# Block one's output projection: divided beside the attention stream, or whole behind it

## The chip, the cores and the metric

One NeuronCore of one Trainium2 chip runs the whole program. The metric is the device time of one execution in microseconds (us), the median of the runs shown. TensorE (PE in the profile) multiplies, VectorE (DVE), ScalarE (ACT) and GpSimd (POOL) do the rest, SyncE (SP) issues the weight loads.

## The reference

Two transformer blocks of two layers each run on 512 tokens of width 1024, in float32. The change lies in block one, whose layer is

```
h    = rmsnorm(x, norm_attn)
proj = h @ w_in
o    = concat(stick_breaking(4 heads), moba(4), nsa(4), diff(4))   # 512 x 1024
x    = x + o @ w_out
x    = x + square(relu(rmsnorm(x, norm_mlp) @ w_up)) @ w_down
```

Block two (SwiGLU, a mixer with pooling, convolution and neighbourhood attention, SwiGLU, each with a layer norm) is the same before and after.

## The kernel before

**Layout.** The activations are held transposed: `xT[:, k, :]` is chunk k of 128 channels by 512 tokens. Each product is done in three matmuls on rounded parts, weight high x input high, weight high x input low, weight low x input high (`three`, L628), so each weight piece (128 x 1024, 8 blocks of 128 x 128) is split: ScalarE copies the high part (`high_for`, L1139), VectorE subtracts for the low part (`split_for`, L1605). Pieces go through four slots in one fixed order; SP loads a piece into its slot when VectorE has split the one before it (L471). `high_for(n)` and `split_for(n)` prepare the piece that follows piece n in its slot. `wait_ge` and `then_inc` on semaphores order the engines; inside an engine all goes in program order.

**The attention stream.** 48 units (head pair and query tile; the width is one to four key tiles of 128) are worked off in 51 steps, an order written out by hand for each engine. At step i TensorE does `scores(i)` (L772), `values(i - 3)` (L811) and `turn(i - 2)`, the transposes (L784). VectorE adds the bias and takes the maximum (`add_bias(i)`, L1760) and scales the exponentials (`weigh(i - 1)`, L1801); ScalarE takes the exponentials (`exponential(i)`, L1253) and copies the transposed probabilities out of PSUM (`turned_out(i - 2)`, L1070). So a unit goes through all three engines and back in three steps. When all units of a stage (a head pair) are done, VectorE copies its output to a chunk of `mixT` (L1805). ScalarE and VectorE then make the chunk's high part (`mix_high`, L1281, at the steps of `HIGH_STEP`) and low part (`mix_low`, L1833, at those of `LOW_STEP`), which the projection reads. The sub-norm of the differential heads' chunks 6 and 7 is the product at L1872.

**The fill.** Between the small matmuls of a step TensorE does large ones. First the last ten pieces of the input projection (`STREAM`), in thirds of 9, 9 and 6 matmuls at the steps of `THIRD_STEP` (L171): the last third, of k5, is at step 37. Then the first part of the output projection at the steps of `HALF_STEP` (L179): for each of eight output chunks d, five of its eight input chunks (`OUT_A`), 15 matmuls in halves of 9 and 6, at steps 40 to 51; the last two halves (step 51) follow the stream. VectorE adds each group to `xT` (`add_group`, L1836), which frees the PSUM bank; two banks, `acc[0]` and `acc[1]`, serve in turn.

**Behind the stream** come eight groups of the other three input chunks (`OUT_B`), 9 matmuls each, each again with an addition. Behind the addition ScalarE and VectorE make the scaled high and low parts (L1325, L1848) that the MLP's first group (`group`, L537, L532 to L534) reads, ScalarE squares the chunk (L1330) and POOL adds the squares (L2202). The weights of the projection are packed on the host in the order of their use (L2326).

Of the kernel before, what the change touches and what calls it, by code (L numbers as in the profile page):

```python
# [25 lines left out]
P = 128  # L26
# [67 lines left out]
GP_MLP = 12 + NC  # L94
# [76 lines left out]
THIRD_STEP = [2 * x for x in range(8)] + [16 + x * 8 // 11 for x in range(11)] + [24 + x * 15 // 11 for x in range(11)]  # L171
# [5 lines left out]
OUT_A, OUT_B = 5, 3  # L177
assert OUT_A + OUT_B == NC
HALF_STEP = [40 + y * 11 // 14 for y in range(2 * NC)]  # L179


def half_from(y):
    return y // 2 * OUT_A + (3 if y % 2 else 0)


def closes_piece(y):
    return half_from(y + 1) // NC > half_from(y) // NC


HIGH_STEP = [37, 37, 38, 38, 39, 47, 47]  # L190
LOW_STEP = [38, 38, 39, 39, 39, 47, 48]
# [20 lines left out]
def emit(nc, x_in, weights, const_in, bucket_in, par1_in, par2_in, table_in, rpb_in, out):  # L212
    with ExitStack() as ctx:
# [3 lines left out]
        def sem(name):  # L217
            return ctx.enter_context(nc.semaphore(name))
# [181 lines left out]
        scaled_hi, scaled_lo, out_done = sem("scaled_hi"), sem("scaled_lo"), sem("out_done")  # L400
# [123 lines left out]
        def _(pe):  # L524
# [109 lines left out]
            def attention(layer):  # L634
# [182 lines left out]
                def out_group(d, order, first_block, first_piece, m):  # L817

                    pe.wait_ge(evacuated[m % 2], gp + m // 2)
                    for n, k in enumerate(order):  # L820
                        block = first_block + n
                        index = R_ATT * SLOTS + first_piece + block // NC
                        if block % NC == 0 or n == 0:
                            pe.wait_ge(split_done, done + (index + 1))
                        if d == 0:
                            pe.wait_ge(mix_lo, layer * NC + (MIX_ORDER.index(k) + 1))
                        w = slice(block % NC * P, (block % NC + 1) * P)
                        mm = three(acc[m % 2][:, :], index % SLOTS, w, k, n == 0, n == len(order) - 1)
                        if block % NC == NC - 1:
                            mm.then_inc(pieces_done, 1)  # L830
                        if n in (2, len(order) - 1):
                            yield
                    if d < NC - 1:
                        mm.then_inc(out_done, 1)

                def first_outs():
                    for d in range(NC):
                        yield from out_group(d, MIX_ORDER[0:OUT_A], d * OUT_A, 0, 24 + d)

                fill, outs = pieces(STREAM), first_outs()  # L840
                for i in range(N_STEPS):
                    if i < N_UNITS:
                        scores(i)
                    thirds, halves = THIRD_STEP.count(i), HALF_STEP.count(i)
                    if thirds > 0:
                        next(fill)
                    elif halves > 0:
                        next(outs)
                    if i >= 3:
                        values(i - 3)  # L850
                    for _ in range(thirds - 1):
                        next(fill)
# [215 lines left out]
        def _(act):  # L1068
# [66 lines left out]
            def attention(layer):  # L1135
# [147 lines left out]
                for i in range(N_STEPS):  # L1283
# [30 lines left out]
                    for y, step in enumerate(HALF_STEP):  # L1314
                        if i == step + 1 and closes_piece(y):
                            high_for(R_ATT * SLOTS + half_from(y) // NC)
                mix_high(NC - 1)
                for y, step in enumerate(HALF_STEP):
                    if step + 1 >= N_STEPS and closes_piece(y):
                        high_for(R_ATT * SLOTS + half_from(y) // NC)  # L1320
                gps = layer * GPS1 + (GP_SETUP + 12 + NC // 2)
                for k in range(NC):
# [9 lines left out]
                    if (k + 1) * OUT_B // NC > k * OUT_B // NC:  # L1332
                        high_for(R_ATT * SLOTS + OUT_A + k * OUT_B // NC)
# [165 lines left out]
        def _(dve):  # L1499
# [101 lines left out]
            def attention(layer):  # L1601
# [234 lines left out]
                def add_group(group):  # L1836
                    m, d = 24 + group, group % NC
                    if d < NC - 1:
                        dve.wait_ge(out_done, layer * (2 * NC - 2) + (group // NC * (NC - 1) + d + 1))
                    else:  # L1840

                        dve.wait_ge(pieces_done, layer * (ROUNDS1 * SLOTS) + R_ATT * SLOTS + (NC if group >= NC else OUT_A))
                    dve.tensor_tensor(xT[:, d, :], acc[m % 2][:, :], xT[:, d, :], ALU.add).then_inc(evacuated[m % 2], 1)  # L1843
# [8 lines left out]
                for i in range(N_STEPS):  # L1852
# [24 lines left out]
                    for y, step in enumerate(HALF_STEP):  # L1877
                        if i == step + 1 and y % 2:
                            add_group(y // 2)
                        if i == step + 2 and closes_piece(y):  # L1880
                            split_for(R_ATT * SLOTS + half_from(y) // NC)
                for y, step in enumerate(HALF_STEP):
                    if y == 2 * NC - 1:
                        mix_low(NC - 1)
                    if step + 1 >= N_STEPS and y % 2:
                        add_group(y // 2)
                    if step + 2 >= N_STEPS and closes_piece(y):
                        split_for(R_ATT * SLOTS + half_from(y) // NC)
# [399 lines left out]
def _pieces(inputs):  # L2288
# [10 lines left out]
    for l in range(DEPTH):  # L2299
# [26 lines left out]
        for order in (MIX_ORDER[0:OUT_A], MIX_ORDER[OUT_A:]):  # L2326
            tiles = [w_out[k * P:(k + 1) * P, d * P:(d + 1) * P] for d in range(NC) for k in order]
            for n in range(0, len(tiles), NC):
                out.append(np.stack(tiles[n:n + NC], 1).reshape(-1))
# [97 lines left out]
```

## Time and profile before

| what | us |
|---|---|
| median of 3 runs (3367.01 to 3369.91) | 3369.19 |
| the profiled execution's own time | 3365.77 |
| its span from first to last instruction | 3363.8 |
| PE busy, of the span | 3278.3 |
| DVE busy | 2049.4 |
| ACT busy | 715.2 |
| POOL busy | 288.7 |
| mean granted TensorE clock | 0.993 |

The profile is of one execution, with times from the first instruction. A row of the timeline gives start and length; neighbouring instructions of one kind are merged (x8), and TensorE's matmuls overlap, so their pace is the distance of their starts, not their length. A number in brackets is the idle time before, with what ended it. Clock 1.00 is 2.4 GHz, 0.50 is 1.2 GHz. The scores of block one (L772) run from 132.6 to 327.4 us in layer one and from 829.0 to 1020.6 in layer two.

### The profile page before, as it was taken

The numbers are of one execution on the slowest core, as the hardware profiler recorded it, in microseconds if no ns is written. First come the engines' busy times: TensorE is split into PE (matmuls) and PEld (weight loads), VectorE is DVE, ScalarE is ACT, GpSimd is POOL, SyncE is SP. The second block draws the span as 40 slices with busy tenths as digits, with TensorE's granted clock in tenths as the row PEclk, the third lists the DMA queues.
The fourth block names the chain that finished last, engine by engine and source line by source line (L and its number), as shares of the span: only waits on it lengthen the run. The fifth ranks groups of instructions, "written<-read, shape, count | busy, mean of one in ns | idle before, by whom it ended". The sixth has DMA issues, their size and how long they took to land.

```text
span 3363.8 us, 44654 instructions
## 1 busy us (share of the span) xinstructions
PE 3278.3 (97%) x15358; PEld 2585.0 (77%) x15358; DVE 2049.4 (61%) x3166; ACT 715.2 (21%) x1419; POOL 288.7 (9%) x224
## 2 busy tenths in 40 slices
PE   8999999999999999999999999999999999999998
PEld 6766788878657888788886778888788867778886
DVE  5676655555776555654457776455745476774547
ACT  3465200014653000100003321000200023320001
POOL 0110100030101000200002410000100014200001
PEclk9999999999999999999999999999999999999999
DMA  5211223224112222232322213222222222222222
GB/s 215 94 45 51 91 94 100 94 76 150 39 57 72 97 97 95 87 99 96 100 81 94 70 63 100 100 95 86 95 94 94 95 79 90 65 86 98 96 95 68
DMA packets 86777, 302.20 MB, mean 90 GB/s; under 512 B 9267, under 2 KB 10035, under 8 KB 86368
## 3 DMA queue, kind: packets, MB, share of 16 engines
q1 hardware_dynamic: 81180, 287.67, 25.5%
q10 hardware_dynamic: 5444, 12.52, 1.1%
q8 instruction: 91, 1.49, 0.2%
q14 instruction: 62, 0.51, 0.0%
HBM read 298.03 MB, written 6.06 MB: 90 GB/s over the span
## 4 chain that ended last, share of the span: by engine, by line
PE 88%; DVE 5%; DVEq 3%; issue 2%; ACT 1%; DMA 1%; POOL 1%; POOLq 0%; ACTq 0%; SPq 0%
PE acc L532 19%; PE acc L534 19%; PE acc L533 19%; PE acc L630 3%; PE acc L631 2%; PE acc L632 2%; PE acc L879 2%; PE acc L881 2%; PE acc L880 2%; PE score L772 2%; PE outp L811 1%; PE trans L784 1%; DVE wL L1509 1%; PE acc L562 1%; PE acc L563 1%
## 5 line engine op out<-in xcount | busy, mean ns | idle before, releaser
L1509 DVE TENSOR_TENSOR wL<-wraw,wH 128x1024 fp32r<-128x1024 f32 x459 | 605.1, 1318 | 34.3
L533 PE MATMUL acc<-opL,wH 128*128 128x512 f32 x1280 | 498.2, 389 | 0.0
L532 PE MATMUL acc<-opH,wH 128*128 128x512 f32 x1280 | 498.2, 389 | 0.0
L534 PE MATMUL acc<-opH,wL 128*128 128x512 f32 x1280 | 498.2, 389 | 0.0
L532 PE MATMUL acc<-hidH,wH 128*128 128x512 f32 x1072 | 417.2, 389 | 0.0
L534 PE MATMUL acc<-hidH,wL 128*128 128x512 f32 x1072 | 417.2, 389 | 0.0
L533 PE MATMUL acc<-hidL,wH 128*128 128x512 f32 x1072 | 417.2, 389 | 0.0
L1507 DVE CAST wH<-wraw 128x1024 fp32r<-128x1024 f32 x459 | 324.8, 708 | 135.4 <-PE acc L534 121.4
L1405 ACT ACTIVATE big<-acc 128x512 f32<-128x512 f32 x84 | 50.5, 601 | 1173.1 <-PE acc L534 1170.2
L534 PEld LDWEIGHTS acc<-opH,wL 128*128 128x128 f32 x1280 | 240.4, 188 | 50.0
L532 PEld LDWEIGHTS acc<-opH,wH 128*128 128x128 f32 x1280 | 240.4, 188 | 49.8
L533 PEld LDWEIGHTS acc<-opL,wH 128*128 128x128 f32 x1280 | 240.4, 188 | 49.5
L1990 DVE TENSOR_TENSOR xT<-acc,xT 128x512 f32 (+1 forms) x128 | 88.3, 690 | 266.2 <-PE acc L534 253.9
L534 PEld LDWEIGHTS acc<-hidH,wL 128*128 128x128 f32 x1072 | 201.3, 188 | 42.0
L533 PEld LDWEIGHTS acc<-hidL,wH 128*128 128x128 f32 x1072 | 201.3, 188 | 41.6
L532 PEld LDWEIGHTS acc<-hidH,wH 128*128 128x128 f32 x1072 | 201.3, 188 | 41.5
L2017 DVE SCALAR_TENSOR_TENSOR big<-acc,big 128x512 f32<-128x512 f32 x84 | 58.0, 691 | 276.1 <-PE acc L534 275.7
L532 PE MATMUL acc<-scaledH,wH 128*128 128x512 f32 x512 | 201.5, 394 | 3.9 <-DVE xT L1843 3.9
L630 PE MATMUL acc<-opH,wH 128*128 128x512 f32 x448 | 189.9, 424 | 11.1 <-DVE xT L1843 5.4
L534 PE MATMUL acc<-scaledH,wL 128*128 128x512 f32 x512 | 200.6, 392 | 0.0
L533 PE MATMUL acc<-scaledL,wH 128*128 128x512 f32 x512 | 200.6, 392 | 0.0
L632 PE MATMUL acc<-opH,wL 128*128 128x512 f32 x448 | 178.3, 398 | 0.0
(310 smaller groups left out, 4955.2 us busy)
## 6 DMA issues: line engine op xcount, KB each, us to landing
wraw<-in_weights SPq DMA_DIRECT2D x507, 512.0 KB, 3.3
wraw<-in_weights SPq DMA_DIRECT2D x32, 384.0 KB, 3.0
big<-bias_scratch ACTq DMA_DIRECT2D x10, 512.0 KB, 3.6
bias_scratch<-bias_rows SPq DMA_DIRECT2D x3, 1280.0 KB
big<-in_par ACTq DMA_DIRECT2D x2, 1536.0 KB, 8.0
big<-in_x SPq DMA_DIRECT2D x4, 512.0 KB, 8.9
mixT<-bias_scratch ACTq DMA_DIRECT2D x2, 1024.0 KB, 7.7
out_x<-big SPq DMA_DIRECT2D x8, 256.0 KB, 2.3
```

Source lines behind the costliest of these rows:

```text
L532: pe.matmul(accum[:, :], wH[:, slot, w], hi[:, k, :], start=k == 0, stop=False)
L533: pe.matmul(accum[:, :], wH[:, slot, w], lo[:, k, :], start=False, stop=False)
L534: mm = pe.matmul(accum[:, :], wL[:, slot, w], hi[:, k, :], start=False, stop=k == n - 1)
L630: pe.matmul(accum, wH[:, slot, w], hi[:, k, :], start=first, stop=False)
L631: pe.matmul(accum, wH[:, slot, w], lo[:, k, :], start=False, stop=False)
L632: return pe.matmul(accum, wL[:, slot, w], hi[:, k, :], start=False, stop=last)
L772: pe.matmul(scp[b][:, 0:width], q[rows_of, x.t * P:(x.t + 1) * P], k[rows_of, 0:width], start=True, stop=True).then_inc(scores_ready, 1)
L879: pe.matmul(accum, wH[:, slot, w], opH[:, k, :], start=k == 0, stop=False)
L880: pe.matmul(accum, wH[:, slot, w], opL[:, k, :], start=False, stop=False)
L1507: dve.tensor_copy(wH[:, slot, :], wraw[:, slot, :])
L1509: dve.tensor_tensor(wL[:, slot, :], wraw[:, slot, :], wH[:, slot, :].bitcast(F32), ALU.subtract).then_inc(split_done, 1)
L1990: ins = dve.tensor_tensor(x, acc[j % 2][:, :], x, ALU.add)
```

## The change

The output projection is no longer divided. Steps 42 to 50 of the stream have no fill. Behind the stream come eight groups of 24 matmuls, one for each output chunk and weight piece, in the order `MIX_ORDER` of the input chunks, with one addition each: eight additions per layer where there were sixteen. The thirds of the last pieces of the input projection are set from `24 + x * 15 // 11` to `24 + x * 17 // 10`, so v5 ends at step 30 (29 before), q5 at 35 (33), k5 at 41 (37). The high and low parts of `mixT` move from steps 37 to 39 to steps 42 to 45, the last ones stay about where they were. The weight pieces of the projection are packed whole, one for each output chunk; their number and size are the same. The semaphore `out_done` goes; the additions wait for `pieces_done`.

```diff
-GP_MLP = 12 + NC
+GP_MLP = 12 + NC // 2
...
-THIRD_STEP = [2 * x for x in range(8)] + [16 + x * 8 // 11 for x in range(11)] + [24 + x * 15 // 11 for x in range(11)]
+THIRD_STEP = [2 * x for x in range(8)] + [16 + x * 8 // 11 for x in range(11)] + [24 + x * 17 // 10 for x in range(11)]
...
-OUT_A, OUT_B = 5, 3
-assert OUT_A + OUT_B == NC
-HALF_STEP = [40 + y * 11 // 14 for y in range(2 * NC)]
...
-HIGH_STEP = [37, 37, 38, 38, 39, 47, 47]
-LOW_STEP = [38, 38, 39, 39, 39, 47, 48]
+HIGH_STEP = [42, 42, 43, 43, 44, 47, 47]
+LOW_STEP = [43, 43, 44, 44, 45, 48, 48]
...
+                def out_group(d):
+
+                    index, m = R_ATT * SLOTS + d, 24 + d
                     pe.wait_ge(evacuated[m % 2], gp + m // 2)
+                    pe.wait_ge(split_done, done + (index + 1))
+                    for n, k in enumerate(MIX_ORDER):
                         if d == 0:
+                            pe.wait_ge(mix_lo, layer * NC + (n + 1))
+                        mm = three(acc[m % 2][:, :], index % SLOTS, slice(n * P, (n + 1) * P), k, n == 0, n == NC - 1)
+                    mm.then_inc(pieces_done, 1)
...
-                    thirds, halves = THIRD_STEP.count(i), HALF_STEP.count(i)
+                    thirds = THIRD_STEP.count(i)
                     if thirds > 0:
                         next(fill)
-                    elif halves > 0:
-                        next(outs)
...
-                    for _ in range(halves if thirds else halves - 1):
-                        next(outs)
...
                 rest_of(fill)
-                rest_of(outs)
                 for d in range(NC):
-                    rest_of(out_group(d, MIX_ORDER[OUT_A:], d * OUT_B, OUT_A, 24 + NC + d))
+                    out_group(d)
...
-                    if (k + 1) * OUT_B // NC > k * OUT_B // NC:
-                        high_for(R_ATT * SLOTS + OUT_A + k * OUT_B // NC)
+                    high_for(R_ATT * SLOTS + k)
...
+                def add_group(d):
+                    m = 24 + d
+                    dve.wait_ge(pieces_done, layer * (ROUNDS1 * SLOTS) + (R_ATT * SLOTS + d + 1))
                     dve.tensor_tensor(xT[:, d, :], acc[m % 2][:, :], xT[:, d, :], ALU.add).then_inc(evacuated[m % 2], 1)
...
+                mix_low(NC - 1)
                 for d in range(NC):
-                    add_group(NC + d)
+                    add_group(d)
                     if d > 0:
                         scaled_low(d - 1)
-                    last = (d + 1) * OUT_B // NC > d * OUT_B // NC
-                    if last and d < NC - 1:
-                        split_for(R_ATT * SLOTS + OUT_A + d * OUT_B // NC)
+                    if d < NC - 1:
+                        split_for(R_ATT * SLOTS + d)
                 scaled_low(NC - 1)
...
+        for d in range(NC):
+            tiles = [w_out[k * P:(k + 1) * P, d * P:(d + 1) * P] for k in MIX_ORDER]
+            out.append(np.stack(tiles, 1).reshape(-1))
```

## Rows read from the trace of the kernel before

**Rows 1.** The page: shares of the chain that ended last, by engine.
```profile
PE 88%; DVE 5%; DVEq 3%; issue 2%; ACT 1%; DMA 1%; POOL 1%; POOLq 0%; ACTq 0%; SPq 0%
```

**Rows 2.** Windows: length, busy (count) of PE, PEld, DVE, ACT, POOL; clock, DMA share, GB/s.
```profile
985.05:1036.64 51.59, 49.84 (x284) 33.63 (x285) 31.65 (x94) 26.09 (x67) 0.00 (x0) 0.97 0.17 52
1036.64:1060.12 23.48, 20.32 (x89) 16.21 (x88) 17.58 (x21) 11.32 (x17) 7.11 (x5) 1.00 0.20 68
1060.12:1067.29 7.17, 7.17 (x25) 5.72 (x26) 5.23 (x5) 3.18 (x5) 3.05 (x2) 0.76 0.30 87
291.70:343.40 51.70, 49.63 (x284) 33.56 (x284) 31.65 (x94) 26.10 (x67) 0.00 (x0) 0.97 0.16 52
366.88:374.03 7.15, 7.15 (x25) 5.72 (x25) 5.32 (x5) 3.27 (x5) 3.06 (x2) 0.76 0.25 83
```

**Rows 3.** Timeline, PE, steps 46 and 47: start, length, engine, line, what [idle before <- releaser].
```profile
1014.47 1.09 PE L784 MATMUL trans<-const,big 128*128 128x128 f32 x8
1015.49 0.92 PE L772 MATMUL score<-big 64*128 64x384 f32 x4
1016.34 0.50 PE L630 MATMUL acc<-opH,wH 128*128 128x512 f32 x1
...
1018.62 1.09 PE L811 MATMUL outp<-big 128*64 128x128 f32 x16
1019.65 0.44 PE L784 MATMUL trans<-const,big 128*128 128x128 f32 x2
1020.01 1.13 PE L772 MATMUL score<-big 64*128 64x512 f32 x4
```

**Rows 4.** Timeline, PE, the divided projection's waits and the first MLP group.
```profile
1030.12 0.50 PE L630 MATMUL acc<-opH,wH 128*128 128x512 f32 x1 [1.52 <-DVE xT L1843]
...
1049.92 0.39 PE L631 MATMUL acc<-opL,wH 128*128 128x512 f32 x1
1050.15 0.39 PE L632 MATMUL acc<-opH,wL 128*128 128x512 f32 x1
1051.70 0.50 PE L630 MATMUL acc<-opH,wH 128*128 128x512 f32 x1 [1.16 <-DVE xT L1843]
...
1060.12 0.47 PE L532 MATMUL acc<-scaledH,wH 128*128 128x512 f32 x1 [2.00 <-DVE xT L1843]
```

**Rows 5.** Timeline, PE, steps 39 and 40.
```profile
983.49 0.40 PE L811 MATMUL outp<-big 128*64 128x128 f32 x2 [1.34 <-ACT big L1070]
...
985.05 1.13 PE L772 MATMUL score<-big 64*128 64x128 f32 x4 [0.78 <-DVE small L1760]
```

**Rows 6.** Windows, steps 38 to 40, columns as in rows 2.
```profile
978.89:982.10 3.21, 3.21 (x18) 1.59 (x17) 1.87 (x9) 2.96 (x6) 0.00 (x0) 1.00 0.01 3
982.10:985.98 3.88, 1.63 (x10) 0.99 (x8) 3.75 (x10) 3.88 (x10) 0.00 (x0) 1.00 0.01 2
986.00:989.30 3.30, 3.20 (x9) 1.98 (x7) 3.15 (x6) 2.01 (x6) 0.00 (x0) 0.50 0.02 5
```

**Rows 7.** Timeline, ACT: projection copy, weight copy, exponential of four tiles, two high parts.
```profile
983.25 0.58 ACT L1070 ACTIVATE big<-acc 128x512 f32<-128x512 f32 x1
983.73 1.05 ACT L1070 ACTIVATE wH<-wraw 128x1024 fp32r<-128x1024 f32 x1
...
1002.75 0.72 ACT L1253 ACTIVATE big<-big,small 128x512 f32<-128x512 f32 x1 [0.55 <-DVE small L1760]
...
1026.23 1.15 ACT L1070 ACTIVATE opH<-mixT 128x512 fp32r<-128x512 f32 x2
```

**Rows 8.** Timeline, DVE: stage copy, sub-norm product, addition, bias of four tiles.
```profile
1019.79 0.69 DVE L1805 TENSOR_SCALAR mixT<-outp 128x512 f32<-128x512 f32 x1 [0.84 <-PE outp L811]
1020.40 0.74 DVE L1872 SCALAR_TENSOR_TENSOR mixT<-mixT,small,rows 128x512 f32<-128x512 f32 x1
...
1022.19 0.69 DVE L1843 TENSOR_TENSOR xT<-acc,xT 128x512 f32<-128x512 f32 x1
1022.79 0.68 DVE L1760 CUSTOM_DVE_ANT_0 big<-score,big 128x512 f32<-128x512 f32 x1
```

More of the change, by code:

```diff
@@ L176 @@
 MIX_ORDER = CHUNK
-OUT_A, OUT_B = 5, 3
-assert OUT_A + OUT_B == NC
-HALF_STEP = [40 + y * 11 // 14 for y in range(2 * NC)]
[L182 to L187, printed above, removed]
-HIGH_STEP = [37, 37, 38, 38, 39, 47, 47]
-LOW_STEP = [38, 38, 39, 39, 39, 47, 48]
+HIGH_STEP = [42, 42, 43, 43, 44, 47, 47]
+LOW_STEP = [43, 43, 44, 44, 45, 48, 48]
 MAPS1 = NORMS1 = TRS1 = 2 * N_UNITS
@@ L399, in emit @@
                                                             sem("tab_set"))
-        scaled_hi, scaled_lo, out_done = sem("scaled_hi"), sem("scaled_lo"), sem("out_done")
+        scaled_hi, scaled_lo = sem("scaled_hi"), sem("scaled_lo")
         squared, summed, rstd_ready = sem("squared"), sem("summed"), sem("rstd_ready")
@@ L815, in values @@
                                 mm.then_inc(pv_done, 2 if x.kind == "diff" else 1)
-                def out_group(d, order, first_block, first_piece, m):
+                def out_group(d):
+                    index, m = R_ATT * SLOTS + d, 24 + d
                     pe.wait_ge(evacuated[m % 2], gp + m // 2)
[L820 to L824, printed above, removed]
-                        if d == 0:
[L826 to L840, printed above, removed]
+                    pe.wait_ge(split_done, done + (index + 1))
+                    for n, k in enumerate(MIX_ORDER):
+                        if d == 0:
+                            pe.wait_ge(mix_lo, layer * NC + (n + 1))
+                        mm = three(acc[m % 2][:, :], index % SLOTS, slice(n * P, (n + 1) * P), k, n == 0, n == NC - 1)
+                    mm.then_inc(pieces_done, 1)
+                fill = pieces(STREAM)
                 for i in range(N_STEPS):
@@ L1313, in attention @@
                             mix_high(n)
-                    for y, step in enumerate(HALF_STEP):
-                        if i == step + 1 and closes_piece(y):
-                            high_for(R_ATT * SLOTS + half_from(y) // NC)
                 mix_high(NC - 1)
[L1318 to L1321, printed above, removed]
+                gps = layer * GPS1 + (GP_SETUP + 12)
                 for k in range(NC):
@@ L1834, in mix_low @@
                                       ).then_inc(mix_lo, 1)
[L1836 to L1842, printed above, removed]
+                def add_group(d):
+                    m = 24 + d
+                    dve.wait_ge(pieces_done, layer * (ROUNDS1 * SLOTS) + (R_ATT * SLOTS + d + 1))
                     dve.tensor_tensor(xT[:, d, :], acc[m % 2][:, :], xT[:, d, :], ALU.add).then_inc(evacuated[m % 2], 1)
@@ L1876, in attention @@
                             mix_low(n)
[L1877 to L1888, printed above, removed]
+                mix_low(NC - 1)
                 for d in range(NC):
-                    add_group(NC + d)
+                    add_group(d)
                     if d > 0:
                         scaled_low(d - 1)
-                    last = (d + 1) * OUT_B // NC > d * OUT_B // NC
-                    if last and d < NC - 1:
-                        split_for(R_ATT * SLOTS + OUT_A + d * OUT_B // NC)
+                    if d < NC - 1:
+                        split_for(R_ATT * SLOTS + d)
                 scaled_low(NC - 1)
@@ L2325, in _pieces @@
         w_out = g["w_out"][l]
[L2326 to L2329, printed above, removed]
+        for d in range(NC):
+            tiles = [w_out[k * P:(k + 1) * P, d * P:(d + 1) * P] for k in MIX_ORDER]
+            out.append(np.stack(tiles, 1).reshape(-1))
         for part in range(PARTS1):
```

## The prediction

> **What bounds the kernel now.** I read the page first. The chain of waits that ended last lies 88% on TensorE [rows 1], so a change pays only where TensorE stands still or runs at its lower clock. Then came the second layer's attention tail by windows (985.05 is the first score of step 40, 1036.64 the end of the last values, 1060.12 the start of the first MLP group), and TensorE's timeline inside them. In steps 40 to 50 (51.59 us) TensorE is busy 49.84 and the mean clock is 0.97; the first layer's copy of it takes 51.70 [rows 2]. So the divided projection already fills the stream, and nearly nothing is left idle there. Behind it come 23.48 us with 20.32 busy, and the first MLP group with 7.17 us at clock 0.76 (7.15 in layer one) [rows 2]. These idle and slow places are what the change can win; what it can lose is the filling.
>
> **The sum is per layer; there are two layers.**
>
> *The work is the same.* The projection is 64 blocks of three matmuls before and after, with the same eight weight pieces. 120 of the 192 matmuls (eight groups of 15, the last 15 already at the stream's end) move from steps 40 to 50 to behind the stream. The SP queue issues the same loads in the same order and VectorE splits the same pieces; only the eight extra additions of 0.69 us go [rows 8], and VectorE isn't what ends the stream while filled, so they alone give nothing.
>
> *Won 1: bank waits.* The fill at 1030.12 waited 1.52 us for an addition queued behind the split and two low parts. The groups of nine are too short for VectorE's additions, splits and scaled low parts: TensorE starts at 1051.70, 1.55 us after the matmul before it where 0.23 is normal (1.3 lost), and at 1060.12 after 2.00 us idle, which with the end of the matmul before it makes 2.2 lost [rows 4]. Undivided groups of 24 last 24 x 0.23 = 5.5 us each against some 3 us of VectorE work (addition, split and scaled low part), and the first MLP group uses the bank freed one group earlier, so all three go: 1.5 + 1.3 + 2.2 = **5.0**.
>
> *Won 2: the clock of the first MLP group.* It took 7.17 us at mean clock 0.76, right behind the 2.00 us idle [rows 2, 4]. At full clock it is 24 x 0.23 = 5.5. The idle is gone, so is the lower clock: **1.7**.
>
> *Won 3: entering and leaving the fill.* A fill of nine in the stream, from 1016.34 to the next values at 1018.62, takes 2.28 us [rows 3]; nine at 0.23 are 2.07. That is 0.2 us for each of 14 separate half groups; they run in one piece after: 14 x 0.2 = 2.8, and I take **2.8**.
>
> *Won 4: steps 36 to 40.* TensorE idles 1.34 us in step 39 and 0.78 before the scores of step 40 [rows 5], because ScalarE does the power, four high parts and a piece there and VectorE three low parts more; then the clock is 0.50 over the 3.30 us in which step 40's fill begins [rows 6], seven of its matmuls at twice their 0.2 us, 1.4 us. The change moves the high and low parts to steps 42 to 45 and sets thirds of a piece at steps 37, 39 and 41. Of 3.5 us I take **3.0**, as the first values after a first scores still wait for ScalarE's copy.
>
> Won in all: 5.0 + 1.7 + 2.8 + 3.0 = 12.5.
>
> *Lost 1: waits in the unfilled steps.* From the last third of the last piece (step 41) to the stream's end nothing covers the chain scores, bias, exponential, weighing, transpose, copy, values. TensorE's own work there: scores of 0.85 for three key tiles (and 1.1 for four), values of 1.03 for four, transposes of 1.02 for four and 0.36 for one, from start to start [rows 3], the other sizes in proportion. Six scores, ten values, nine transposes and one head sum come to about 19 us. Three places wait, by my count:
> (a) Steps 42 to 44. ScalarE, in order: two exponentials (1.2, an estimate from the 0.72 for four tiles), copies of probabilities (0.4), the projection copy 0.58, the weight copy 1.05, two high parts 1.15, two exponentials at 0.72, copies 0.6 [rows 7]: 6.4 us. TensorE has 2.7 of its own beside it and starts 0.2 later: wait 3.5.
> (b) Steps 46 to 48. VectorE: two biases over three tiles (1.1, from 0.68 for one over four), weighing (1.1, an estimate), a stage copy 0.69 and the sub-norm product 0.74 (1.3 from start to start), one bias 0.6 [rows 8], then ScalarE's two exponentials 1.4 and copies 0.6: 6.1 us. TensorE has 2.3 beside it and enters some 0.8 later: wait 3.0.
> (c) Steps 48 to 50 have no scores and end in copy and values by turns, and ScalarE has two high parts (1.15) more: 2.0 in all.
> Together **8.5**. Bounds: VectorE's own busy time is 31.65 in steps 40 to 50 [rows 2]; without six additions (4.1), step 40 and the splits that leave, with five low parts that come in, some 23 remain against TensorE's 19, so at least 4. The nearest row without fill is 978.89 to 985.98: 7.1 us, of which TensorE is busy 3.21 + 1.63 = 4.84 [rows 6], 32% idle; on 19 us of work that makes 9, and 12 if the moved high and low parts fall worse. So 4 to 12.
>
> *Lost 2: the clock.* With waits like (a) and (b) the clock can fall again. The trace shows both cases. From 978.89 to 982.10 nothing but small matmuls run, with no idle time, and the clock stays 1.00; from 982.10 to 985.98 TensorE is busy 1.63 of 3.88 us, still at 1.00, and behind it the clock is 0.50 [rows 6]. One such spell in small work costs 0.8 to 1.4, since part of it lies in a wait that was there anyway; one over dense matmuls 1.7 (Won 2). I expect (a) or (b) to bring one spell in the stream and (b) with (c) one at the head of the projection: 1.2 + 1.7 = **2.9**. Bounds: 0, and the whole unfilled stretch at 0.50, which doubles the 19 us but swallows the waits: about 10, plus 1.7 behind it.
>
> *The head of the projection costs nothing:* group 0 has 21 matmuls (4.8 us) before it needs the last stage's low part, about 3 us after the last values (1036.64, by rows 2, to a copy, a high and a low part). Nor does its foot: the last addition, scaled high and low parts take some 2.5 us, under the first 21 matmuls of the MLP group; the squares' sum on POOL ends inside it.
>
> Sum: 8.5 + 2.9 - 12.5 = -1.1 per layer, -2.2 for both; I round to **-2.5 us**. The profiled execution took 3365.77 us (span 3363.8); the median of the runs shown is 3369.19, 3.4 above it. On the median that gives **3366.7 us**. A measurement of this kernel can tell about 0.2% (6.7 us) from no change.
>
> **Rivals.**
> *A, the waits stay small and the clock stays up (faster).* Waits at 6, no spell in the stream, half of one behind it: 12.5 - 6 - 0.9 = 5.6 per layer, 11 us, 3358; at the low bound 3352. For it: small matmuls alone kept the clock at 1.00 [rows 6]. Against: single waits of over 2 us, and 1.63 of 3.88 busy was enough for a fall. It decides from about 2.3 us less loss per layer than I count.
> *B, the clock stays low through the unfilled steps (slower).* Several falls between steps 42 and 50, say two thirds of the stretch: 6.7 plus 1.7 behind, waits 8.5: 16.9 - 12.5 = +4.4 per layer, 9 us, 3378; the full bound gives +7.7, 15 us, 3384. It decides from 7 us of clock loss per layer, about six spells in small work. For it: the fall at 985.98 came right after the only two neighbouring steps without fill; the change makes nine. Against: after 982.10 the clock was still whole.
> The Trainium skill ("TensorE: Matmul & The Clock Gate", "A second HAM failure mode: psum-queue depth-cycling") says that frequent short idles between groups of matmuls make the clock swing and cost throughput, which speaks against this change and for B; no wait in this trace's filled stream is frequent enough to show it.
> *C, the high and low parts cost more than (a) says.* Each stage of the chain queues behind them in steps 42 to 45; at the upper bound of 12 us of waits with two spells: +2.4 per layer, 5 us, 3374. That is still within 0.2%.
>
> **How the numbers follow.** Forecast with C: 0.48, of which 0.03 lies beyond 0.2% on the faster side. A: 0.30. B: 0.22. So faster 0.33, same 0.45, slower 0.22. The range goes from A's middle to beyond B's beginning, 3355 to 3377; the forecast's own is 3361 to 3374.
>
> **What would show it.** Right: the additions in the projection 5.5 us apart with no wait of TensorE between them and none before the first MLP group, that group near 5.5 us at clock 1.00; the stream from the start of step 40 to the last values some 31 to 34 us instead of 51.6, two single waits of 2 to 3 us before values in steps 44 and 48; one or two half-clock spells per layer. Wrong for A: TensorE idle under 6 us in the unfilled steps. Wrong for B: a mean clock under 0.75 over them. Anything that differs past the first MLP group of a layer would make the whole ledger wrong.

## The result, and the profile after

The changed kernel took 3374.09 us (median of 13 runs) against 3368.13 us of the kernel before beside it: ratio 1.0017, 95% interval 1.0010 to 1.0025. A second comparison of the same two (after_again, below) gave 3375.21 against 3366.88 us, ratio 1.0023, 1.0014 to 1.0032. The change costs 6 to 8 us. The forecast was a gain of 2.5. Two of the 13 runs of the changed kernel took 4638 and 5750 us at a mean clock of 0.75 and 0.71; they aren't in the ratio, and without them the median is 3373.83.

The page of the changed kernel, its span, TensorE's busy time and the shares of the chain that ended last:

```profile
span 3371.2 us, 44584 instructions
...
PE 3283.6 (97%) x15358; PEld 2592.5 (77%) x15358; DVE 2037.7 (60%) x3150; ACT 714.1 (21%) x1419; POOL 285.9 (8%) x224
...
PE 88%; DVE 4%; DVEq 3%; issue 2%; ACT 2%; DMA 1%; POOL 1%; ACTq 0%; POOLq 0%; SPq 0%
```

TensorE still makes 88% of the chain, as in [rows 1], and it is busy 5.3 us longer than before (3283.6 against 3278.3) although it does the same matmuls. More busy time for the same work is a first sign of a lower clock, and the mean granted clock agrees: 0.989 in this profile, 0.993 in that of before.

Windows of the changed kernel: length, busy (count) of PE, PEld, DVE, ACT, POOL, clock, DMA share, GB/s. Layer two first: steps 24 to 27, step 40 to the last values, the projection, the first MLP group; then the first three of these of layer one.

```profile
920.58:946.00 25.42, 20.23 (x96) 12.59 (x95) 18.19 (x40) 15.40 (x33) 4.16 (x2) 0.73 0.18 60
986.90:1022.24 35.34, 28.57 (x186) 18.41 (x185) 24.08 (x82) 23.20 (x65) 0.00 (x0) 0.83 0.11 31
1022.24:1067.34 45.10, 44.63 (x195) 36.64 (x193) 21.01 (x23) 15.99 (x22) 7.72 (x6) 0.98 0.21 71
1067.34:1072.91 5.57, 5.57 (x25) 4.58 (x26) 3.26 (x4) 2.19 (x3) 1.34 (x1) 1.00 0.33 104
225.17:249.58 24.41, 19.20 (x97) 11.69 (x96) 18.21 (x40) 15.29 (x33) 4.16 (x2) 0.79 0.19 62
288.94:322.25 33.31, 26.42 (x186) 17.04 (x185) 24.01 (x82) 23.20 (x65) 0.00 (x0) 0.90 0.11 33
322.25:366.56 44.31, 43.85 (x195) 35.99 (x193) 21.01 (x23) 16.00 (x22) 7.73 (x6) 1.00 0.22 73
```

Windows of the kernel before, steps 24 to 27 in layer one and layer two, which the prediction did not look at:

```profile
224.97:248.01 23.04, 17.73 (x96) 11.30 (x95) 15.12 (x33) 13.77 (x30) 4.15 (x2) 0.85 0.19 63
921.40:941.38 19.98, 16.05 (x96) 10.26 (x95) 15.16 (x33) 13.80 (x30) 4.16 (x2) 0.91 0.22 74
```

The second to fourth rows answer to the first three of [rows 2]. The stream from step 40 on shrank from 51.59 to 35.34 us, the projection grew from 23.48 to 45.10, the first MLP group fell from 7.17 to 5.57 at clock 1.00. The price stands in the clock column: from step 40 to the last values 0.97 before, 0.83 now (0.90 in layer one); the first window, steps 24 to 27, is at 0.73 and 0.79 where before it had 0.91 and 0.85.

| stretch, us, layer one / layer two | before | after | after_again | after_warm2 (a run below, clock held) |
|---|---|---|---|---|
| start of step 24 to 28 | 23.0 / 20.0 | 24.4 / 25.4 | 24.4 / 25.4 | 20.3 / 20.2 |
| step 28 to 40 | 43.7 / 43.7 | 39.4 / 40.9 | 39.3 / 40.8 | 41.4 / 39.8 |
| step 40 to the last values | 51.7 / 51.6 | 33.3 / 35.3 | 35.6 / 35.3 | 30.9 / 30.9 |
| from there to the MLP | 23.4 / 23.5 | 44.3 / 45.1 | 45.9 / 45.2 | 44.4 / 44.3 |
| first MLP group | 7.2 / 7.2 | 5.5 / 5.6 | 5.6 / 5.6 | 5.6 / 5.6 |
| sum | 149.1 / 145.9 | 146.9 / 152.3 | 150.7 / 152.2 | 142.5 / 140.9 |

The 41.4 of layer one in the last column holds a spell of half clock (mean clock 0.96 there, against none in layer two's 39.8).

From step 28 on the change gives near nothing (before 126.0 / 125.9, after 122.5 / 126.9), close to what was foretold, but by errors that cancel (below). Steps 24 to 27 add 1.4 and 5.4 us. The two layers together are 4.3 us longer in this profile, 8.0 in the second one. What is left of the spans' difference in this profile, 3.1 us, is more half clock outside the changed stretches: a clock of 0.82 over the 19 us from 724 us on, where before had 0.91 over 721 to 740, and 0.89 against 1.00 from 1950 to 1965. Profiles of kernels that lose nothing have such spells there too (one_third the first, warm_mlp the second), so whether they belong to the change stays open.

TensorE's timeline in steps 44 to 50 of layer two of the changed kernel (start, length, engine, line, what, in brackets the idle time before and what ended it):

```profile
996.00 0.44 PE L798 MATMUL outp<-big 128*64 128x128 f32 x4 [0.44 <-DVE mixT L1768]
...
999.94 0.97 PE L798 MATMUL outp<-big 128*64 128x128 f32 x8 [2.29 <-ACT big L1040]
...
1010.12 0.44 PE L798 MATMUL outp<-big 128*64 128x128 f32 x4 [0.36 <-DVE mixT L1768]
...
1013.40 0.78 PE L798 MATMUL outp<-big 128*64 128x128 f32 x8 [2.25 <-ACT big L1040]
...
1016.23 1.55 PE L798 MATMUL outp<-big 128*64 128x128 f32 x12 [0.58 <-ACT big L1040]
...
1020.37 1.97 PE L798 MATMUL outp<-big 128*64 128x128 f32 x16 [0.69 <-ACT big L1040]
1022.27 0.80 PE L617 MATMUL acc<-opH,wH 128*128 128x512 f32 x1
```

Two single waits of 2.3 us stand before the values of steps 44 and 48, where the prediction put them; all six make 6.6 us. Behind the second everything runs at half clock: 16 values take 1.97 us here and 1.09 in [rows 3], and the projection's first matmuls still run at that pace. Such a wait doesn't bring a fall every time. In layer one of the same profile the wait of step 44 is as long, and the eight values behind it take 0.66 us, where the half clock makes 0.97 of them above:

```profile
301.97 0.66 PE L798 MATMUL outp<-big 128*64 128x128 f32 x8 [2.28 <-ACT big L1040]
```

Behind the stream, VectorE's last two additions (L1802) and TensorE's first MLP matmul of the changed kernel:

```profile
1061.47 0.69 DVE L1802 TENSOR_TENSOR xT<-acc,xT 128x512 f32<-128x512 f32 x1 [0.90 <-PE acc L619]
...
1066.91 0.69 DVE L1802 TENSOR_TENSOR xT<-acc,xT 128x512 f32<-128x512 f32 x1 [0.89 <-PE acc L619]
```
```profile
1067.34 0.47 PE L519 MATMUL acc<-scaledH,wH 128*128 128x512 f32 x1 [0.47 <-issue]
```

The additions are 5.44 us apart and now VectorE waits for TensorE. The waits of 1.16 and 2.00 us of [rows 4] are gone; 0.47 us without a named cause is left before the MLP.

What happens in steps 24 to 27 of layer two of the changed kernel, TensorE's timeline:

```profile
933.14 1.94 PE L771 MATMUL trans<-const,big 128*128 128x128 f32 x8 [3.02 <-ACT big L1231]
935.02 1.65 PE L759 MATMUL score<-mixT 32*128 32x384 f32 x4
936.60 1.98 PE L798 MATMUL outp<-big 128*64 128x128 f32 x16
...
938.91 2.08 PE L759 MATMUL score<-mixT 32*128 32x512 f32 x4
940.92 0.80 PE L617 MATMUL acc<-opH,wH 128*128 128x512 f32 x1
```

A wait of 3.02 us, then 7.8 us of small matmuls back to back at half clock. TensorE is never idle in them, and the clock does not come back; here it comes back only in the fill that begins at 940.92. Before, a third of v5 stood in step 26, inside this stretch; the new spacing puts it in step 27.

### The profile page after: what moved, and what is told of

Same layout as the page of the kernel before. It is cut to its first block, busy times and chain, and to the rows that moved or that the text cites. A ratio compares the mean times of both kernels' runs of the same rounds, so it can differ in the third digit from the quotient of the medians.

```text
span 3371.2 us, 44584 instructions
## 1 busy us (share of the span) xinstructions
PE 3283.6 (97%) x15358; PEld 2592.5 (77%) x15358; DVE 2037.7 (60%) x3150; ACT 714.1 (21%) x1419; POOL 285.9 (8%) x224
## 3 DMA queue, kind: packets, MB, share of 16 engines
q1 hardware_dynamic: 81180, 287.67, 25.4%
## 4 chain that ended last, share of the span: by engine, by line
PE 88%; DVE 4%; DVEq 3%; issue 2%; ACT 2%; DMA 1%; POOL 1%; ACTq 0%; POOLq 0%; SPq 0%
PE acc L519 19%; PE acc L521 19%; PE acc L520 19%; PE acc L617 3%; PE acc L618 2%; PE acc L619 2%; PE acc L849 2%; PE acc L851 2%; PE acc L850 2%; PE score L759 2%; PE outp L798 2%; PE trans L771 1%; DVE wL L1472 1%; PE acc L549 1%; PE acc L550 1%
## 5 line engine op out<-in xcount | busy, mean ns | idle before, releaser
L1470 DVE CAST wH<-wraw 128x1024 fp32r<-128x1024 f32 x459 | 323.9, 706 | 134.9 <-PE acc L521 120.6
## 6 DMA issues: line engine op xcount, KB each, us to landing
mixT<-bias_scratch ACTq DMA_DIRECT2D x2, 1024.0 KB, 7.6
```

Of the source, the lines that this page charges most:

```text
L1470: dve.tensor_copy(wH[:, slot, :], wraw[:, slot, :])
```

## The experiments

The idle-time matmuls in some of these kernels are extra: they go to a PSUM bank that is free just then and nothing reads them. The rest of the computation is unchanged.

**Hold the clock in the two long waits.** The changed kernel, and:

```diff
+                def warm_gap(count):
+                    pe.wait_ge(evacuated[0], gp + 12)
+                    pe.wait_ge(split_done, done + (R_ATT * SLOTS + 1))
+                    for _ in range(count):
+                        pe.matmul(acc[0][:, :], wH[:, 0, 0:P], wH[:, 0, 0:SEQ], start=True, stop=True)
...
                     if thirds > 0:
                         next(fill)
+                    if i in (44, 48):
+                        warm_gap(9)
                     if i >= 3:
                         values(i - 3)
```

> The undivided kernel with nine matmuls on weights into an idle bank (no part of the result) in front of the values of steps 44 and 48, where TensorE waits 2.29 and 2.25 us. They last 2.1 us and fit the wait. Theory Clock: no fall of the clock behind steps 44 and 48 any more; half-clock time from step 40 to the last values goes from 6.8 and 11.9 us to 0 to 3.4, and 2 to 4 us are won over the two layers against the changed kernel (3370 to 3372). Rival Chain: the clock there costs nothing, since the waits are ScalarE's and VectorE's; the time is the changed kernel's, or up to 1 us more where the nine matmuls end after the wait.

Measured: 3361.45 us (11 runs), ratio to the kernel before 0.9983 (0.9974 to 0.9991), 12.6 us below the changed kernel's 3374.09 and far more than the 2 to 4 us expected. Windows as above, step 40 to the last values of layer one and layer two:

```profile
288.16:319.06 30.90, 28.11 (x204) 18.24 (x203) 23.99 (x82) 23.01 (x65) 0.00 (x0) 1.00 0.12 35
982.08:1012.99 30.91, 28.12 (x204) 18.23 (x203) 23.99 (x82) 23.01 (x65) 0.00 (x0) 1.00 0.12 35
```

The clock is 1.00, and the stretch falls from 33.31 and 35.34 to 30.90 and 30.91 us with 18 matmuls more in it. ScalarE's and VectorE's busy times hardly change. So the waits are the chain's own, and what they cost beyond themselves is the clock. The table's five stretches account for 8.7 us of the profiles' 11.8; the rest is the half clock near 730 and 1959 us, which is less here. Undivided, with the clock held here, is faster than the kernel before.

**Is the new spacing of the thirds to blame?** The changed kernel with the old spacing, and the kernel before with one third of v5 moved from step 26 to 27:

```diff
-THIRD_STEP = ... + [24 + x * 17 // 10 for x in range(11)]
+THIRD_STEP = ... + [24 + x * 15 // 11 for x in range(11)]
```

> The undivided kernel with the thirds of the last ten pieces at the steps of the kernel before (24 + x * 15 // 11), high and low parts as changed. Theory Clock (the third that left step 26 is what keeps TensorE at 0.50 in steps 24 to 28: 24.40 and 25.42 us against 23.05 and 19.98): steps 24 to 28 go back to 20 to 23 us in both layers, and the time falls by 3 to 7 us against the changed kernel, to 3367 to 3371, level with the kernel before. Rival Chain (the loss is the waits of steps 42 to 50, the spells in steps 24 to 28 are chance): the median stays within 2 us of the changed kernel's 3374; without the thirds at 39 and 41 steps 38 to 41 have more waits, so it may be 1 to 3 us above it.

```diff
-THIRD_STEP = ... + [24 + x * 15 // 11 for x in range(11)]
+THIRD_STEP = ... + [24 + x * 15 // 11 + (x == 2) for x in range(11)]
```

> The kernel before, with nothing changed but one third of v5 moved from step 26 to step 27. Theory Clock: the low spell that begins in step 25 lasts 10 us and more instead of 3.4 to 6.8, so steps 24 to 28 take 24 to 26 us in a layer instead of 20 to 23, and the median rises by 3 to 7 us over the kernel before. Rival Chain: the work is the same and step 26 to 28 only trade places: within 1.5 us of the kernel before, and steps 24 to 28 of the profile within 1 us of 20 to 23.

Measured: thirds_back 3371.63 us (12 runs), ratio 1.0010 (1.0001 to 1.0019); one_third 3368.54 us (11 runs), ratio 1.0002 (0.9993 to 1.0011). Windows of steps 24 to 27, layer one and two, thirds_back first, then one_third:

```profile
224.07:245.59 21.52, 16.20 (x96) 10.18 (x95) 15.13 (x33) 13.78 (x30) 4.15 (x2) 0.92 0.22 70
923.01:947.05 24.04, 18.69 (x97) 12.09 (x96) 15.16 (x33) 13.93 (x30) 4.15 (x2) 0.79 0.19 62
```
```profile
223.56:243.75 20.19, 16.05 (x96) 10.24 (x95) 16.39 (x39) 15.16 (x33) 4.16 (x2) 0.92 0.23 75
918.38:943.84 25.46, 20.25 (x96) 12.58 (x96) 18.19 (x40) 15.41 (x33) 4.15 (x2) 0.73 0.18 58
```

The same code takes 20.19 us in one layer and 25.46 in the other, by where the clock falls. Over all profiles with the third in step 27 (the changed kernel twice, one_third, warm_44_48: eight layers) the stretch takes 24.3 us in the mean, over those with it in step 26 and nothing else changed there (before, thirds_back, warm_mlp: six layers) 22.2. That points to 2 us per layer, but both intervals reach to nearly nothing, and thirds_back fell between its two expectations, so the share of the spacing stays unsettled between 0 and about 4 us. By the medians 4.2 of the 6 to 8 us remain with the old spacing, and the single third costs the kernel before 1.1 us, which is within the noise: the spacing alone does not explain the loss.

**The spell in steps 24 to 27 by itself.** The kernel before with idle-time matmuls in step 24 and 25. The first attempt wrote them to `acc[1]`:

```diff
+                def warm_25(count):
+                    pe.wait_ge(evacuated[1], gp + 10)
+                    for _ in range(count):
+                        pe.matmul(acc[1][:, :], opH[:, 0, 0:P], opH[:, 0, :], start=True, stop=True)
...
+                    if i in {24: 4, 25: 8}:
+                        warm_25({24: 4, 25: 8}[i])
                     if 2 <= i < N_UNITS + 2:
                         turn(i - 2)
```

> The kernel before with idle-time matmuls in steps 24 and 25: four before the transposes of step 24, where TensorE stands 1.12 us in the profile of before, and eight before those of step 25, where it stands 1.88 us. They write a free accumulator bank and nothing reads them. Clock theory (the spell of half clock in steps 24 to 28, 6.8 us long in layer one and 3.4 in layer two of the profile of before, comes from these idle places and varies by chance with them): steps 24 to 28 take 18 to 19 us in both layers instead of 23.05 and 19.98, no half clock in them, and the median falls by 3 to 8 us (ratio 0.9976 to 0.999). Rival (the spell comes from the small matmuls, which count too little whether or not the gaps are filled): the spell stays and the time is the same or up to 2 us longer.

Measured: 3367.77 us (11 runs), ratio 0.9997 (0.9988 to 1.0007). The rival's number, but not for its reason, as TensorE's timeline shows:

```profile
927.71 1.57 PE L843 MATMUL acc<-opH 128*128 128x512 f32 x4 [1.50 <-ACT big L1077]
929.08 1.48 PE L784 MATMUL trans<-const,big 128*128 128x128 f32 x6
```

The added matmuls themselves waited 1.50 us, for ScalarE's copy out of `acc[1]`: a new idle place in the old one's stead. The second attempt takes the transposes' bank, which is free between values and transposes, so it waits for nothing:

```diff
+                def warm_25(count):
+                    for _ in range(count):
+                        pe.matmul(trp[0][:, :], opH[:, 0, 0:P], opH[:, 0, :], start=True, stop=True)
```

> warm_25 without its own new wait: the four and eight idle-time matmuls of steps 24 and 25 now write the transposes' bank, which is free between values and transposes, so that they wait for nothing (in warm_25 they waited 1.50 us for ScalarE's copy out of the accumulator, and the values' row at 925.55 came no earlier). Clock theory: no half clock in steps 24 to 28, which take 18 to 19.5 us in both layers instead of 23.05 and 19.98; the median falls by 2 to 8 us (ratio 0.9976 to 0.9994). Rival (the spell has another cause than these two idle places): the spell stays, the ratio is within 0.0005 of 1.

Measured: 3362.88 us (11 runs) against 3366.88, ratio 0.9983 (0.9974 to 0.9993). Windows of steps 24 to 27, both layers:

```profile
225.36:245.40 20.04, 17.80 (x109) 11.49 (x108) 15.19 (x33) 13.81 (x30) 4.20 (x2) 1.00 0.23 73
918.70:938.73 20.03, 17.82 (x109) 11.48 (x108) 15.18 (x33) 13.80 (x30) 4.20 (x2) 1.00 0.21 74
```

No half clock, and the two layers are alike within 0.01 us. The kernel before thus carried a loss of 4.0 us there in its median. The floor of 20.0 is a little above the 18 to 19.5 expected: the 3 us gap of step 25 stays, with eight idle-time matmuls and a wait of 1.0 us in it.

**Both places held in the changed kernel**, first with the same faulty wait (after_warm), then without (after_warm2: warm_44_48 with 4 and 12 matmuls into `trp[0]` in steps 24 and 25).

> The changed kernel with matmuls in the waits of steps 44 and 48 (nine each, as in warm_44_48) and also in steps 24 and 25 (3, 4 and 12, before the waits of 0.78, 1.11 and 3.01 us). Clock theory: no half clock from step 24 to the MLP in either layer, steps 24 to 28 take 18 to 19 us instead of 24.4, the median 9 to 13 us below warm_44_48's 3361.4: 3348 to 3352. It shows what the undivided projection is worth when the clock is held everywhere; if the divided one with the clock held (three_warm) is still lower, the filling itself, not only the clock, is worth something. Rival (the spell in steps 24 to 28 doesn't come from the idle places): 3360 to 3363.

> warm_44_48 with 4 and 12 idle-time matmuls in steps 24 and 25 between values and transposes, waiting for nothing. Steps 24 to 28 take 19 to 21 us instead of 24.4 in both layers, no half clock in them; the median 3352 to 3357 against warm_44_48's 3361.4. It is what the undivided projection gives with the clock held in the stream. Rival: the half clock in steps 24 to 28 covers waits that are there anyway, 3360 to 3362.

Measured: after_warm 3362.76 us (11 runs), ratio 0.9984 (0.9975 to 0.9993), a miss for the reason of warm_25: its own wait at step 24 was 2.94 us long. after_warm2 3354.39 us (5 runs), ratio 0.9960 (0.9946 to 0.9975), inside its expectation. Its steps 24 to 27 in layer two (layer one is alike):

```profile
916.02:936.26 20.24, 18.70 (x112) 12.24 (x111) 16.44 (x39) 15.18 (x33) 4.20 (x2) 1.00 0.22 73
```

Against the changed kernel beside it (3375.21) that is 20.8 us, 10 per layer, all from 34 extra matmuls per layer.

**The first MLP group alone (Won 2).** The kernel before with eight idle-time matmuls into `trp[0]` ahead of that group's wait.

> The kernel before with eight matmuls on a free bank ahead of the first MLP group, where TensorE stands 2.00 us. It tests Won 2 alone. If the half clock of that group comes from the idle before it, the group takes 5.5 us instead of 7.15 in both layers, clock 1.00 there, and the median falls by about 3.3 us (ratio 0.999). If it comes from the waits further up (1.16 us before the sixth group) the group stays at 7.15 and the time is the same.

Measured: 3366.14 us (11 runs), ratio 0.9999 (0.9990 to 1.0008): the expected 3.3 us is not resolved. The windows of the group, both layers, are clear:

```profile
366.51:371.96 5.45, 5.45 (x26) 4.51 (x26) 5.19 (x5) 3.14 (x5) 3.07 (x2) 1.00 0.30 96
1062.04:1067.53 5.49, 5.49 (x26) 4.51 (x25) 5.20 (x5) 3.14 (x5) 3.07 (x2) 1.00 0.25 96
```

5.45 and 5.49 us instead of 7.15 and 7.17 [rows 2]: the group's low clock came from the idle time right before it.

**The changed kernel once more.**

> The changed kernel once more, for a second profile and a second comparison. If the loss is systematic, the ratio is again above 1.000 with a median 4 to 8 us above before; steps 40 to the last values again hold 7 to 14 us of half clock in each layer (6.8 and 11.9 in the first profile), the first MLP group again has none. If the first result was chance in where the clock falls, the ratio comes out at 0.999 to 1.0005 and the half clock in these steps differs by a factor of two or more.

Measured: 3375.21 us (11 runs), ratio 1.0023. Windows of this second profile, steps 24 to 27 and step 40 to the last values of layer one, then of layer two:

```profile
226.27:250.70 24.43, 19.21 (x97) 11.75 (x96) 18.20 (x40) 15.30 (x33) 4.15 (x2) 0.79 0.18 62
290.01:325.58 35.57, 28.66 (x186) 18.30 (x185) 24.11 (x82) 23.20 (x65) 0.00 (x0) 0.81 0.11 31
...
925.42:950.79 25.37, 20.14 (x97) 12.58 (x96) 18.21 (x40) 15.42 (x33) 4.15 (x2) 0.73 0.19 61
991.62:1026.92 35.30, 28.52 (x186) 18.38 (x185) 24.11 (x82) 23.22 (x65) 0.00 (x0) 0.83 0.10 31
```

The loss is systematic. Only layer one differs from the first profile, from step 40 on (0.81 against 0.90 in the unfilled steps).

**A middle way.** The kernel before, divided three to five, each of the eight first groups a whole fill of nine, the moved high and low parts spread wide:

```diff
-OUT_A, OUT_B = 5, 3
+OUT_A, OUT_B = 3, 5
-HALF_STEP = [40 + y * 11 // 14 for y in range(2 * NC)]
+HALF_STEP = [40, 41, 43, 44, 45, 47, 48, 50]
-HIGH_STEP = [37, 37, 38, 38, 39, 47, 47]
-LOW_STEP = [38, 38, 39, 39, 39, 47, 48]
+HIGH_STEP = [37, 37, 38, 40, 41, 46, 48]
+LOW_STEP = [38, 38, 39, 44, 45, 48, 50]
-... [24 + x * 15 // 11 for x in range(11)]
+... [24, 24, 26, 27, 29, 30, 32, 33, 34, 35, 37]
```

> The kernel before with the projection divided three chunks to five (fill of 9 matmuls at steps 40, 41, 43, 44, 45, 47, 48, 50; eight groups of 15 behind the stream), high parts at 37, 37, 38, 40, 41, 46, 48, low parts at 38, 38, 39, 44, 45, 48, 50, and thirds at 24, 24, 26, 27, 29, 30, 32, 33, 34, 35, 37. If what the ledger says holds (bank waits of the groups of nine 3.5 us, the slow first MLP group 1.7 us, waits and spell of steps 39 and 40 some 3 us per layer, all gone without the waits of the unfilled steps), it is 10 to 20 us faster than the kernel before: 3348 to 3358, with the first MLP group at 5.5 us. If the clock falls in the thinner stream all the same (fills of 9 instead of up to 15 in a step), 0 to 5 us faster.

> three_first with idle-time matmuls at its waits: 3 and 4 in step 24, 6 and 12 in step 25, 5 before the values of step 39 (waits of 0.78, 1.12, 1.59, 3.01 and 1.34 us in its profile). Clock theory: no half clock from step 24 to the MLP; steps 24 to 28 take 18 to 19 us instead of 25.5, steps 28 to the end of the last values about 3 us less than 83.2; in all some 9 us per layer in the profile, the median at 3337 to 3346 against three_first's 3355.5. Rival (the added matmuls delay the chain of scores, exponentials and values as much as they save): 3352 to 3358.

> three_first with idle-time matmuls that wait for nothing: 4 in step 24 and 12 in step 25 between values and transposes (waits of 1.12 and 3.01 us there), 5 before the values of step 39. three_warm lost by its own wait of 2.94 us in step 24. Clock theory: no half clock from step 24 to the MLP, steps 24 to 28 take 21.5 to 23 us instead of 25.5, the median 3347 to 3352, against three_first's 3355.5. Rival (three_first is bounded there by ScalarE, POOL and VectorE, so that the half clock costs nothing): 3354 to 3358.

Measured: three_first 3355.53 us (5 runs), ratio 0.9964 (0.9951 to 0.9976); three_warm 3359.22 us (8 runs), ratio 0.9975 (0.9965 to 0.9986), worse by its own wait again; three_warm2 3349.84 us (5 runs), ratio 0.9944 (0.9930 to 0.9958). Windows of three_warm2: steps 24 to 27 of layer one; step 40 to the last values of layer one and two; layer two's rest of the projection.

```profile
225.09:247.17 22.08, 20.50 (x122) 14.01 (x121) 17.63 (x39) 15.18 (x33) 4.19 (x2) 1.00 0.26 85
...
287.61:331.84 44.23, 42.65 (x251) 28.12 (x251) 30.13 (x93) 23.93 (x65) 0.00 (x0) 0.92 0.14 43
...
976.04:1018.27 42.23, 40.01 (x251) 26.77 (x251) 30.15 (x93) 23.93 (x65) 0.00 (x0) 1.00 0.14 46
1018.27:1046.36 28.09, 27.53 (x123) 22.48 (x121) 17.92 (x22) 14.11 (x20) 7.97 (x6) 1.00 0.24 83
```

It beats both kernels, the one before by 17 us. Groups of 15 behind the stream are long enough for VectorE (TensorE is busy 27.53 of 28.09 us, where it was 20.32 of 23.48 in [rows 2]), and a fill of nine in eight of the eleven last steps holds the clock by itself. The 6.8 us of half clock left in layer one (clock 0.92, against 1.00 in layer two) show that five matmuls at step 39 don't hold it every time. With the clock held in both, but for that spell and the one in after_warm2's layer one, keeping a part of the projection in the stream is worth 4.5 us over none (3349.84 against 3354.39).

## Why the prediction was wrong

The step that failed is **Lost 2, the clock**, a term of the right kind and mis-sized. It was put at 2.9 us per layer, and only for steps 42 to the head of the projection; the runs show about 8 in its place, with the kernel before's own loss in steps 24 to 27 taken off.

From step 40 on, measured against the held clock (30.9 and 44.3 us in warm_44_48), the changed kernel lost 2.4 and 5.2 us in its first profile and 6.2 and 5.3 in the second: 4.8 in the mean. Two more places, which the prediction priced at nothing, fell to half clock as well: steps 24 to 27, 24.4 and 25.4 us against 20.2 held, 4.7 in the mean where the kernel before lost some 2 (its median gained 4.0 from warm_25b); and a spell behind step 31 of layer two, 1.5 us (40.9 against 39.4 in layer one). Together that is 10 us per layer, or 8 with the kernel before's 2 taken off. The direct experiment, which removes the first two, gives 20.8 us for both layers. The spells were also longer than the one length that was priced: in the changed kernel's layer two the half clock lasts some 10 us behind the wait of step 48 and more than that from step 25 on.

**Without the clock the ledger was nearly right, in part by luck.** 8.5 lost against 12.5 won, 4.0 per layer, 8 for both, was to be what the change gives when the clock costs nothing. after_warm2 against warm_25b, the clock held in both where it was lost in the stream, gives 3354.39 - 3362.88 = -8.5 us. (The half clock at step 40 and in the first MLP group of before stays in warm_25b; the ledger counts it under what is won. after_warm2 keeps a spell of 1.5 us in layer one.) From step 28 to the end of the first MLP group after_warm2 takes 122.2 us in layer one and 120.6 in layer two, against 126.0 and 125.9 before: a gain of 3.8 and 5.3, and of 5.3 in both but for that spell. The waits were counted 1.9 us too long and the gains some 0.8 too high. With the waits too long by 1.9 us and the clock from step 40 on too short by as much (4.8 for 2.9), the sum from step 28 on came out near its forecast by chance; what tipped the result is steps 24 to 27, for which the sum had no term.

Term by term. *Won 1*: right in kind, some 4.4 us instead of 5.0; the additions are 5.44 us apart where 5.5 was said, but the first MLP matmul starts 0.86 us after the one before it, 0.6 more than the pace. *Won 2*: right, 7.15 and 7.17 to 5.52 and 5.57, and warm_mlp shows that the idle before it was the cause. *Won 3 and 4*: not measured one by one. By difference they come to about 5.7 where 5.8 was said: the gain of 5.3, plus 6.4 for the waits of after_warm2 and the 18 idle-time matmuls in them, less 4.4 and 1.6 for Won 1 and 2. *Lost 1*: right in its places, too large in size: (a) 2.7 us instead of 3.5, (b) 2.6 instead of 3.0, (c) 1.3 instead of 2.0, together 6.6 instead of 8.5. *Head and foot of the projection*: no wait for the last stage's low part, as foretold. Of the signs that were named, the stream from step 40 on was to take 31 to 34 us: it took 33.3 to 35.6 as changed and 30.9 with the clock held.

**Which reading led to it.** The prediction read in [rows 6] that small matmuls alone, TensorE never idle, kept the clock at 1.00 from 978.89 to 982.10, and took the two long waits for the only danger. The changed kernel shows the contrary in steps 31 and 32, where no wait is over 0.3 us:

```profile
955.69 1.13 PE L759 MATMUL score<-mixT 32*128 32x512 f32 x4
956.75 0.43 PE L798 MATMUL outp<-big 128*64 128x128 f32 x2
957.11 0.44 PE L771 MATMUL trans<-const,big 128*128 128x128 f32 x2
957.70 1.09 PE L759 MATMUL score<-mixT 32*128 32x128 f32 x4
958.73 0.50 PE L617 MATMUL acc<-opH,wH 128*128 128x512 f32 x1
959.06 0.52 PE L618 MATMUL acc<-opL,wH 128*128 128x512 f32 x1
959.38 0.63 PE L619 MATMUL acc<-opH,wL 128*128 128x512 f32 x1
```

The clock falls at 959.2, right behind these short, busy matmuls, and the fill pays for it. And at 933.14 (above) such matmuls do not bring it back. In [rows 6] the same kind of stretch happened to hold, as it does in steps 31 and 32 of layer one; one good place was not evidence for nine unfilled steps. The second error was to give each spell one short length. With no fill behind it a spell can go on through the steps that follow, as behind step 48; it need not, since after the wait of step 44 full clock is back by 1004.45, where twelve values take 0.88 us. The fill in these steps did two things, it used TensorE's gaps and it kept its clock up, and only the first was in the ledger.

**The rivals.** B was the right mechanism, in a smaller size than its text: from step 42 to the last values the mean clock was 0.88 and 0.80, in the second profile 0.78 and 0.80, not under 0.75, and the missing part of the loss lay in steps 24 to 27. The Trainium skill's rule that was quoted for it ("TensorE: Matmul & The Clock Gate", "A second HAM failure mode: psum-queue depth-cycling", on frequent short idles between groups of matmuls) fits only in direction: the clock did swing here, with 10 us of half clock in layer two between 1013.8 and 1024.0. But it was not the short idles that counted: warm_44_48 keeps waits of 0.4 to 0.8 us in these steps and has clock 1.00; filling the two of 2.3 us was enough. A failed by the clock alone: its waits were nearly right (6.6 for 6). C is excluded, the waits were fewer than counted.

## What to carry to other kernels

A filler between small matmuls also holds the clock. Before it is taken out, read the granted clock in every stretch that will stand without it, in both layers and if possible in two profiles, and bound the price of a spell by its going on until the next dense stretch. If it must go, a few matmuls whose result nothing reads, placed in the waits and onto a bank that needs no wait of its own, give the time back (34 per layer, 20.8 us). A divided product should be cut so that each part is longer than the evacuation behind it: 15 matmuls were, 9 were not.

## What the runs showed of the hardware beyond that

The clock's spells can differ between two runs, and between two layers of one run, with the same code, and cost 0 to 5 us each time: steps 24 to 27 of one_third took 20.19 and 25.46 us within one execution. Differences of some microseconds between two profiles are therefore no evidence, unless the granted clock stands beside them.

A float32 subtraction on VectorE can nearly stand still while GpSimd adds. VectorE's timeline of the changed kernel, then GpSimd's, then ScalarE's:

```profile
929.52 3.41 DVE L1572 TENSOR_TENSOR wL<-wraw,wH 128x1024 fp32r<-128x1024 f32 x1 [0.19 <-issue]
```
```profile
923.01 1.81 POOL L2145 TENSOR_TENSOR big<-big 128x768 f32<-128x768 f32 x1 [5.20 <-DVEq L1739]
929.50 2.35 POOL L2145 TENSOR_TENSOR big<-big 128x1024 f32<-128x1024 f32 x1 [4.68 <-DVEq L1739]
```
```profile
931.94 1.06 ACT L1231 ACTIVATE big<-big 128x1024 f32<-128x1024 f32 x1 [2.74 <-POOL big L2145]
```

Of the 80 splits at L1572 in the changed kernel's profile, the 56 that run beside no GpSimd instruction take 1.16 to 1.23 us. Of the 24 others, the 22 beside the additions of L2145 and L2149 grow with the overlap: 1.53 us at 0.45 us of it, 1.81 at 0.73, 3.41 at 2.33. The two beside the additions of L2137 take only 1.45, though these run beside all of them; why is open. The addition doesn't seem to suffer: those of L2145 take 0.73 us for 256 columns and 1.81 for 768 with nothing on VectorE beside them, 1.28 for 512 and 2.35 for 1024 beside a split, each 256 columns some 0.54 more. No run removes the overlap by itself.

This slow split is not what TensorE waits for in step 25, where the long spell of steps 24 to 27 begins. That wait of 3.0 us ends with the exponentials on ScalarE (931.94 to 933.00), which waited for GpSimd's addition, which waited for VectorE's scans; the split ran beside them.
